# A two-lane transformer kernel whose residual stream is kept token by feature, with the down and output weights moving 512 columns at a time

## The reference, cut to what matters

```python
def rms_norm(x, g, eps=1e-6):
    y = x * rsqrt(mean(x * x, axis=-1) + eps)
    return y * g

def first_block(...):                       # each sublayer, in essence
    h = h + rms_norm(mixer_or_ffn(rms_norm(h, g_pre)), g_post)

def modulated_norm(h, g, m, k):
    return rmsnorm(h, g) * (1.0 + m[..., k + 1, :]) + m[..., k, :]

def gated_residual(h, y, g, m, k, weight):
    return h + weight * m[..., k + 2, :] * rmsnorm(y, g)

def swiglu_2(h, w_in, w_out):
    gate, up = split(h @ w_in, 2)
    return (silu(gate) * up) @ w_out        # hidden width 2816 = 22 tiles of 128
```

## Time and profile before

| | |
|---|---|
| median of 3 runs | 2696.52 us (2694.02 to 2698.24) |
| the profiled execution | 2697.63 us |
| its span, first to last instruction | 2695.9 us |
| TensorE busy | 2507.8 us, 93% |
| TensorE weight loads | 2368.0 us, 88% |
| VectorE busy | 1706.4 us, 63% |
| ScalarE busy | 1242.5 us, 46% |
| DMA moved | 480.09 MB, mean 178 GB/s |
| mean granted TensorE clock | 0.969 of full |

### The profile page before, as it was taken

One profiled execution on the slowest core, in us unless ns is written; L12 is line 12 of the kernel. 1 busy time (PEld: TensorE's weight loads), 2 busy tenths in 40 slices (PEclk: granted clock), 3 DMA queues, 4 the chain that ended last, 5 costly groups with the idle time before them and its releaser, 6 DMA issues.

```text
span 2695.9 us, 48269 instructions
## 1 busy us (share of the span) xinstructions
PE 2507.8 (93%) x20500; PEld 2368.0 (88%) x20500; DVE 1706.4 (63%) x2804; ACT 1242.5 (46%) x1687; POOL 1.2 (0%) x6
## 2 busy tenths in 40 slices
PE   5799997899999999999998999999999999787998
PEld 5689996788998898999797999999999999766997
DVE  5565565456766656566777667577575558656655
ACT  4443352344545445455455544464444345444443
POOL 0000000000000000000000000000000000000000
PEclk9899998899999999999898999999999999898999
DMA  5456655623555665544362344455545555363453
GB/s 213 180 194 255 240 198 223 246 104 119 188 186 206 232 252 188 176 152 159 118 202 80 122 157 172 170 189 174 187 171 177 185 173 187 118 235 125 172 180 117
DMA packets 71588, 480.09 MB, mean 178 GB/s; under 512 B 8784, under 2 KB 9296, under 8 KB 17744
## 3 DMA queue, kind: packets, MB, share of 16 engines
q1 hardware_dynamic: 66240, 468.74, 48.9%
q10 hardware_dynamic: 5136, 8.28, 1.0%
HBM read 471.48 MB, written 1.05 MB: 175 GB/s over the span
## 4 chain that ended last, share of the span: by engine, by line
PE 75%; DVE 12%; ACT 6%; DMA 4%; issue 3%; ACTq 0%; DVEq 0%
PE bank L265 65%; ACT whi L224 3%; DMA raw<-w_main 2%; DVE wlo L244 2%; PE bank L302 2%; PE bank L1163 2%; DVE wlo L231 2%; PE bank L1045 1%; DMA raw<-w_down 1%; PE bank L983 1%; DVE HX L685 1%; DVE ARX L734 1%; DVE tmpx L679 1%; PE bank L1033 1%; DMA tmpx<-ARX 0%
## 5 line engine op out<-in xcount | busy, mean ns | idle before, releaser
L265 PE MATMUL bank<-HNX_hi,whi 128*128 128x256 f32 x2872 | 832.9, 291 | 46.0 <-DVE wlo L244 19.1
L224 ACT ACTIVATE whi<-raw 128x2048 fp32r<-128x2048 f32 (+1 forms) x378 | 705.6, 1868 | 337.5 <-PE bank L265 154.5
L265 PE MATMUL bank<-HNX_hi,wlo 128*128 128x256 f32 x2872 | 819.4, 286 | 0.0
L231 DVE TENSOR_TENSOR wlo<-raw,whi 128x1024 fp32r<-128x1024 f32 (+1 forms) x378 | 453.4, 1199 | 561.6 <-ACT whi L224 560.8
L265 PE MATMUL bank<-HNX_lo,whi 128*128 128x256 f32 x2872 | 804.8, 286 | 0.0
L265 PEld LDWEIGHTS bank<-HNX_hi,whi 128*128 128x128 f32 x2872 | 560.5, 195 | 71.3 <-issue 39.4
L265 PEld LDWEIGHTS bank<-HNX_hi,wlo 128*128 128x128 f32 x2872 | 561.1, 195 | 0.0
L265 PEld LDWEIGHTS bank<-HNX_lo,whi 128*128 128x128 f32 x2872 | 552.0, 195 | 0.7 <-issue 0.5
L244 DVE TENSOR_TENSOR wlo<-raw,whi 128x1024 fp32r<-128x1024 f32 (+1 forms) x378 | 451.2, 1194 | 0.0
L265 PE MATMUL bank<-HNC_hi,whi 128*128 128x256 f32 x1280 | 372.8, 291 | 8.4 <-DVE tmpc L496 5.3
L265 PE MATMUL bank<-HNC_lo,whi 128*128 128x256 f32 x1280 | 365.1, 285 | 0.0
(11 more groups left out here) (363 smaller groups left out, 2923.7 us busy)
## 6 DMA issues: line engine op xcount, KB each, us to landing
raw<-w_main SPq DMA_DIRECT2D x270, 1024.0 KB, 4.8
raw<-w_ada SPq DMA_DIRECT2D x72, 1024.0 KB, 4.8
raw<-w_down SPq DMA_DIRECT2D x72, 1024.0 KB, 4.9
raw<-w_down SPq DMA_DIRECT2D x36, 768.0 KB, 4.2
raw<-w_cmp SPq DMA_DIRECT2D x4, 1024.0 KB, 5.7
tmpx<-ARX ACTq DMA_DIRECT2D x18, 128.0 KB, 5.3
tmpx<-ARX ACTq DMA_DIRECT2D x32, 64.0 KB, 4.8
HX<-x_in SPq DMA_DIRECT2D x2, 512.0 KB, 5.8
```

What stands on the lines that cost most here:

```text
L224: NS.activation(WHI[q % HIS][:, 0:size], RAW[m % SLOTS][:, 0:size], ACT.Copy).then_inc(sems["w_hi"], 1)
L231: NV.tensor_tensor(WLO[m % SLOTS][:, 0:half], RAW[m % SLOTS][:, 0:half], WHI[q % HIS][:, 0:half].bitcast(fp32), SUB)
L265: return NT.matmul(dst, (WHI[ordinal[n] % HIS], WLO[n % SLOTS])[w][:, k * 2 * P + col:k * 2 * P + col + P], x[xp][:, kx, :], start=start, ...
```

## The change

The residual streams, and the outputs of all down and output projections, are stored token by feature: `HX` and `HC` are [128, 2, 1024], partition p and index m holding token 128m + p. Layouts of the input, the output, the down weights and the output-projection weights on the host follow.

- The down blocks of both lanes and the four blocks of each output projection (`mix_out`, new) go through `token_tiles`, now with any activation tiles: two halves h of 512 output features; each half has the banks of the two token tiles m, and six down blocks (2, 4, 4, 4, 4, 4 hidden tiles) or two output blocks. The context lane has two blocks for each half and chunk, and uses both its banks, 6 and 7, for each half.
- `put_out` is gone. For half 0 of an output `put_first` squares 512 columns with an accumulated row sum (ACT, `square_rows`), adds the mean's constant (DVE, `half_mean`), and multiplies by the row of post factors (DVE, `gained`). Half 1 is left in its banks for `norm` (`tail`).
- `norm` has per-token factors in one column of a small tile `STAT` and no sums over partitions. It forms the residual first, squares it, takes a second root, scales, turns each pair of feature tiles with four PE transposes (L702), and applies gain and shift behind them. Between these steps the latent lane yields once, 2.2, ahead of the transposes.
- Post factors are rows: `GROW`, [128, 1024] for each lane, filled by a broadcast DMA on POOL's queue (`grow`), from `gain_rows` for the first block and from a DRAM scratch `GSCR` for the second. `gate_row` writes that scratch for the three gate rows of each adaLN layer.
- FFN, `linear`, adaLN rows and attention are otherwise as before; the number of blocks and their bytes are the same.

The core of it, in the diff:

```diff
-CHUNKS = ((0, 8), (8, 16), (16, 22))
-SHORT_FIRST = ((0, 6), (6, 14), (14, 22))
+CHUNKS = ((0, 4, 8), (8, 12, 16), (16, 20, 22))
+SHORT_FIRST = (0, 2, 6, 10, 14, 18, 22)
...
-        HX, HC = sb("HX", [P, KD, T]), sb("HC", [P, KD, T])
+        HX, HC = sb("HX", [P, 2, D]), sb("HC", [P, 2, D])
...
+            def square_rows(S, src, at, junk, *ready):
+                sq = up(f"{S.tag}_sq")
+                if on(act, *ready):
+                    NS.activation(junk, src, ACT.Square, accum_out=S.STAT[:, at:at + 1]).then_inc(sq.sem, 1)
+                return sq
...
+            def gained(S, h, m, src, sq):
+                ev, cols = up(f"{S.tag}_gained"), slice(h * 2 * T, (h + 1) * 2 * T)
+                if on(dve, sq, grown[S.tag]):
+                    NV.tensor_tensor(S.Y[:, m, cols], src, S.GROW[:, cols], MUL).then_inc(ev.sem, 1)
+                return ev
...
-                        for mp in range(4):
-                            banks = S.tiles[2 * (mp % 2)], S.tiles[2 * (mp % 2) + 1]
-                            for cc, (k0, k1) in enumerate(SHORT_FIRST):
...
-                                yield from two_tiles(S, n, [b[:, 0:T] for b in banks], S.G, ks, cc == 0, cc == 2, waits, tile, 2, mp == 3 and cc == 2)
+                        for h in range(2):
+                            banks, tile = S.tiles[2 * h:2 * h + 2], up(f"{t}_tile")
+                            for cc, (k0, k1) in enumerate(zip(SHORT_FIRST, SHORT_FIRST[1:])):
...
+                                yield from token_tiles(S, n, banks, S.G, ks, cc == 0, k1 == KF, waits, tile if k1 == KF else None, h == 1 and k1 == KF)
...
+                    for h in range(2):
+                        for a, b in ((k0, k_mid), (k_mid, k1)):
+                            yield ("D",)
...
+                            if a == k0:
+                                settle(S)
+                                on(pe, *(free.get(x.name) for x in S.pair))
...
             def norm(S, post, pre, mod=None, ready=None, opening=False, then=None):
...
-                    yield ("L", 8.0 if S.lag else 3.5)
-                    tot_y = add_up(S, S.YY, sum_y, 0, now(f"{t}_sq_sum"), *ready)
...
+                    yield from pause(S, 3.0)
+                    for m, (part, first, bank, src, done_) in enumerate(last):
+                        sqs.append(square_rows(S, src, 2 * m + 1, spare(S, m, 1), done_))
+                        if not S.lag:
+                            roots[m] = root_of(S, 2 * m + 1, ST[:, 4 + m:5 + m], 6 + m, sqs[m], part)
...
+                        inv = inverse(S, 6 + m, *roots[m])
+                        for h in range(2):
...
+                                NV.scalar_tensor_tensor(S.H[:, m, HALF[h]], S.Y[:, m, HALF[h]], ST[:, 6 + m:7 + m], S.H[:, m, HALF[h]], MUL, ADD)\
...
+                                NV.tensor_scalar(S.Y[:, m, HALF[h]], S.H[:, m, HALF[h]], ST[:, 14 + m:15 + m], None, MUL).then_inc(sc.sem, 1)
+                yield ("L", 2.0 if S.lag else 2.2)
...
+                for kk in range(4):
+                    bank, turned = S.turns[kk], up(f"{t}_turned")
...
+                                mm = NT.transpose(bank[:, j * T + m * P:j * T + (m + 1) * P], S.Y[:, m, k * P:(k + 1) * P], ident)
...
+                                NV.tensor_scalar(tmp, src, gain(k), shift(k), MUL, ADD).then_inc(no.sem, 1)
...
+                    yield from pause(S, 4.0)
```

More of the change, by code:

```diff
@@ L77 @@
     pair: Any
-    sums: Any
-    wide_y: Any
-    wide_h: Any
+    turns: Any
     chunked: bool
@@ L465, in linear, with mix_out, job, ffn @@
                 return marks
-            def ffn(S, which, gain, first):
+            def mix_out(S, name, ready):
+                parts, firsts = {}, {}
+                for h in range(2):
+                    banks, tile = S.tiles[2 * h:2 * h + 2], up(f"{S.tag}_tile")
+                    for c in range(2):
+                        yield ("D",)
+                        n = take(S.tag, "w_main", MAIN[name] + 2 * h + c)
+                        if c == 0:
+                            settle(S)
+                            on(pe, *ready, *(free.get(b.name) for b in banks))
+                        yield from token_tiles(S, n, banks, S.HN, [(k, 4 * c + k) for k in range(4)], c == 0, c == 1, None, tile if c else None, h == 1 and c == 1)
+                    if h:
+                        tail[S.tag] = [(parts[m], firsts[m], banks[m], banks[m][:, :], done(n) if m else tile) for m in range(2)]
+                        continue
+                    def job(n=n, banks=banks, tile=tile):
+                        for m in range(2):
+                            parts[m], firsts[m] = put_first(S, m, banks[m][:, :], done(n) if m else tile)
+                            free[banks[m].name] = firsts[m]
+                    after(S, job)
+            def ffn(S, which, gain, first, rows=None):
                 t, base, lo_marks = S.tag, MAIN[f"gu{which}"], {}
@@ L644, in norm, with inverse @@
+            def inverse(S, dst, root, inv):
+                if on(dve, root):
+                    NV.reciprocal(S.STAT[:, dst:dst + 1], S.STAT[:, dst:dst + 1]).then_inc(inv.sem, 1)
+                return inv
+            def norm(S, post, pre, mod=None, ready=None, opening=False, then=None):
+                t, ST = S.tag, S.STAT
+                HALF = [slice(h * 2 * T, (h + 1) * 2 * T) for h in range(2)]
+                back, roots = {}, {}
                 if post:
+                    last = tail.pop(t)
@@ new lines, in norm @@
+                    yield from pause(S, 2.0)
+                    evs = []
+                    for m, (part, first, bank, src, done_) in enumerate(last):
+                        if S.lag:
+                            roots[m] = root_of(S, 2 * m + 1, ST[:, 4 + m:5 + m], 6 + m, sqs[m], part)
+                        evs.append(gained(S, 1, m, src, sqs[m]))
+                        if bank is not None:
+                            free[bank.name] = evs[m]
+                    yield from pause(S, 2.0)
```

633 lines of the change are left out of this document (276 added, 357 removed).

## The result

The changed kernel takes 2710.5 us (median of 5, 2706.8 to 2714.8) against 2698.2 for the kernel before beside it. The ratio is 1.0052 (95%: 1.0040 to 1.0065), so slower beyond doubt, where 2660 and a gain were forecast.

The account below looks back on a forecast made before the run. TensorE, busy 93% of the span, was taken as the bound, its idle time sitting in the joints. Terms -37 - 35 + 17 - 2 + 6 + 9 + 5 = -37 us gave 2660 us, range 2630 to 2688.

Parts of the forecast that it names:

- Dense part: Down and output projections: 2,856 pairs of 256-column matmuls become single 512-column ones, 0.013 us saved each, -37 us.
- Uncovered joints and the end: Norms without other work beside them, opening and end: shorter chain, first projection after about 9.6 us, together -35 us.
- Covered joints: Five latent norms filled by other blocks: fewer pauses, 5.8 us idle each against 2.4 before, +17 us.
- The sixth, thinly covered one: Joint from FFN 2 to attention, already 5.8 us idle: loses two trips between engines, -2 us.
- Transposes: On TensorE in ten covered norms, replacing sums and spreads: 1.7 against some 1.2 us a norm, +6 us.
- Context down blocks: Each half uses both banks and needs both evacuated before the next; uncovered in the attention, +5 us.
- Attention of layer 0: Context norm comes later, behind nine score groups instead of six: three more softmax waits of 3 us, +9 us.
- The slower rival: Five covered norms lose their cover, TensorE idling ahead of the transposes: +67 us instead of +17, 2711 us; chance 0.09.

Follow-up runs that it names:

- x_halves: The changed kernel with each 512-column matmul of the token-by-feature products issued as two of 256 columns: 2740.4 us, ratio 1.0162.
- x_open_c: Changed kernel with latent-norm pauses put back, opening and table loads reordered, and the context norm's pause ahead of its transposes raised from 2.0 to 4.0: 2652.5 us.
- x_late: Changed kernel plus ten context half blocks owed after the latent norms ahead of FFN 2 and FFN 4, done in the dense stretches behind them: 2687.4 us.
- x_dup: The changed kernel with each transpose of the norms issued twice, 240 more: 2711.8 us, ratio 1.0058.
- x_open: Changed kernel with latent-norm pauses put back, opening reciprocals and scalings ahead of the first split, and root table loads ahead of ScalarE's wait before two attentions: 2660.3 us.

## Why the prediction was wrong

- **Dense part, -37:** right. -37.1 by the ledger, at least three quarters of the spacing's worth by x_halves. "Loads stay the same in number" holds for the DMA blocks only: TensorE's weight loads fell with its matmuls, 20500 to 17462. The Trainium skill's rule for isolated matmuls ("TensorE: Matmul & The Clock Gate", section "Back-to-back issue gap") would have left an estimated 7 us; x_halves, with 30 us for 3,096 pairs, disagrees.
- **Uncovered joints and the end, -35:** -26 (-2.7, -8.0, -6.8, -1.9, -6.6). The direction was right, the chain laid out too short: 13.2 us where 9.6 was worked out, in front of the last attention. I took the table load as hidden and the transposes as lying beside the scalings, and in the opening I overlooked that the reciprocals stood behind a split that waits for the first weights. The end came to 8.0 us against 8.1.
- **Covered joints, +17 and their share of +6:** +26.4 with their transposes, some 7 us more than the 17 and half of the 6. In idle time alone 5.0, 6.0, 6.0, 4.8 and 5.1 where 5.8 was worked out: the idle time was right. The sixth, thinly covered one (-2) gave -5.0.
- **Transposes:** counted at 6 us as work on TensorE; the doubling (240 more for 1 us) shows that they lie in time that is lost anyway.
- **Context down blocks, +5:** idle in front of them rose by 5.6. Outside the joints the stages other than the two attentions lost 15 altogether, 22 in the FFN stages. The remainder is not taken apart; the context norm's wait for its scalings, which x_open_c removes, is 1.2 us in the changed kernel and explains little of it.
- **Attention of layer 0, +9, and what the lag costs elsewhere, nothing:** this is the step that failed. I had counted in the order that the context lane came three score groups later, and priced that as three waits on softmax at one place. Those waits came as priced: four more, 14.6 us instead of 5.9, so +8.7. But the count was a symptom: the pauses that I had written down as gone were where the context lane made its progress, so it is late at both attentions. The rest of the attention of layer 0 grew by 19, and the last one, which I had booked as an uncovered joint with nothing else to lose, by 17, without one softmax wait more. 36 us instead of 9, and x_late gets 40 of them back by bringing the context lane forward while the norms keep their two half blocks.

Added up, the 46 us between -37 and +9 are the two attentions (27), the uncovered joints and the end (9), the covered joints (7, less 3 in the sixth), and some 6 in the other stages.

The slower rival had the mechanism's first half, and its 2711 us is the measured time, but that is luck: it put 67 us into the five covered joints, which lost 26. It left out what x_late shows, the delay handed on. The argument should have asked: how many half blocks of cover are removed (eight for each of five norms), where are they done instead, and which wait did they fill there before? Its chance of 0.09 was too low, since a pause taken out of five norms was in the diff.

What stays open: the part of the FFN stages named above, how much of the attentions' 36 us beyond 16 of idle time is lost and how much is small work that changed its stage, and how far 46 us divide into cover and lag in the kernel with pauses, since the two were not varied independently there; about 20 for the lag (x_late) and the remainder for the joints is a difference of two kernels.

## What to carry to other kernels

When two lanes share an engine, a filler block is worth something only where the other lane waits; an edit that shortens a chain but removes its pauses also moves the filler's own progress, and the bill comes at the next stage that relies on it. Count in the new order how much of the other lane is done at each later wait, and price those waits. Before judging a new data layout, give it the old layout's cover: with pauses put back the changed kernel gained 46 us and beat the old one by 1.2%, and the pauses were worth 70 us to the old kernel.

## What the runs showed of the hardware

- On operands split for f32r a matmul of 512 columns cost 0.227 us and one of 256 columns 0.120, each with its weight load: the median distance of two starts, over the changed kernel's 3,096 and the old kernel's 17,208.
- TensorE work put into a wait can be nearly free: 240 more transposes (x_dup) cost 1 us, and the mean granted clock went from 0.961 to 0.969. Behind a wait of 9 us transposes took 0.21 us each, at a granted clock of 0.50, which is the 1.2 GHz level; behind a busy stretch 0.107.
- A table load of 1.28 us stands in the chain when ScalarE waits for a matmul ahead of it: 2.2 us from the start of the last matmul to the first square in front of the last attention, where without it (x_open) it is 0.8 us.
